# A streaming encoder's opening norm: the row scale moved from a ScalarE copy into the matmul that transposes the rows

## What is computed

```python
def _rms_norm(x, g):
    xf = x.astype(jnp.float32)
    y = xf * lax.rsqrt(jnp.mean(xf * xf, axis=-1, keepdims=True) + EPS)
    return (y * g.astype(jnp.float32)).astype(x.dtype)

h = _rms_norm(x, g_pre_mix)
z = h @ w_in
```

## Time and profile before

| what | us |
|---|---|
| median of 3 runs | 2531.35 |
| lowest and highest of them | 2529.56, 2534.56 |
| profiled execution, its own time | 2537.56 |
| its span in the trace | 2535.8 |
| third part of block 0 starts (end of the opening) | 41.41 |

### The profile page before, as it was taken

One profiled execution on the slowest core, in us unless ns is written; L12 is line 12 of the kernel. 1 busy time (PEld: TensorE's weight loads), 2 busy tenths in 40 slices (PEclk: granted clock), 3 DMA queues, 4 the chain that ended last, 5 costly groups with the idle time before them and its releaser, 6 DMA issues.

```text
span 2535.8 us, 37474 instructions
## 1 busy us (share of the span) xinstructions
PE 2475.6 (98%) x14264; PEld 2354.4 (93%) x14264; DVE 1158.1 (46%) x2297; ACT 674.4 (27%) x1365; POOL 490.3 (19%) x729
## 2 busy tenths in 40 slices
PE   7999999999999999999999999999999999999998
PEld 6999999999989999999999999988899898898996
DVE  4052425233366556557656435555343343343335
ACT  5122222323222222222222322323022131131221
POOL 1021201121165445446436000001000000000000
PEclk9999999999999999999999999999999999999999
DMA  4252625353423313322422634322011021110114
GB/s 160 90 183 73 222 78 180 119 172 122 138 76 132 126 58 123 128 85 95 136 96 97 219 124 133 100 91 83 25 59 42 25 66 33 33 58 25 49 41 157
DMA packets 219182, 256.88 MB, mean 101 GB/s; under 512 B 8256, under 2 KB 186816, under 8 KB 218944
## 3 DMA queue, kind: packets, MB, share of 16 engines
q1 hardware_dynamic: 219072, 255.37, 30.6%
HBM read 175.12 MB, written 80.22 MB: 101 GB/s over the span
## 4 chain that ended last, share of the span: by engine, by line
PE 70%; issue 12%; DVE 12%; DMA 2%; POOL 2%; ACT 1%; SPq 1%; DVEq 0%; POOLq 0%; ACTq 0%
PE bank L596 9%; PE bank L598 9%; PE bank L597 9%; PE bank L826 5%; PE bank L828 5%; PE bank L827 5%; PE bank L896 5%; PE bank L897 5%; PE bank L895 5%; PE bank L747 3%; DVE QE L1377 2%; DVE PP L1380 2%; PE bank L854 1%; PE bank L855 1%; PE bank L856 1%
## 5 line engine op out<-in xcount | busy, mean ns | idle before, releaser
L596 PE MATMUL bank<-XH,WHI 128*128 128x384 f32 x2304 | 791.6, 344 | 9.9 <-DVE XL L1242 4.3
L598 PE MATMUL bank<-XH,WLO 128*128 128x384 f32 x2304 | 774.2, 336 | 0.0
L597 PE MATMUL bank<-XL,WHI 128*128 128x384 f32 x2304 | 774.1, 336 | 0.0
L596 PEld LDWEIGHTS bank<-XH,WHI 128*128 128x128 f32 x2304 | 436.6, 190 | 16.0 <-ACT XH L911 6.2
L597 PEld LDWEIGHTS bank<-XL,WHI 128*128 128x128 f32 x2304 | 436.3, 189 | 0.9
L598 PEld LDWEIGHTS bank<-XH,WLO 128*128 128x128 f32 x2304 | 435.4, 189 | 0.0
L911 ACT ACTIVATE ZST<-bank 128x384 f32<-128x384 f32 x240 | 117.9, 492 | 566.3 <-PE bank L598 564.5
L826 PE MATMUL bank<-XH,WHI 128*128 128x384 f32 x768 | 257.7, 335 | 3.6 <-ACT XH L911 3.6
L828 PE MATMUL bank<-XH,WLO 128*128 128x384 f32 x768 | 257.2, 335 | 0.0
L827 PE MATMUL bank<-XL,WHI 128*128 128x384 f32 x768 | 257.2, 335 | 0.0
L1212 DVE TENSOR_TENSOR WLO<-WRAW,WHI 128x1024 fp32r<-128x1024 f32 x128 | 157.5, 1231 | 210.3 <-ACT WHI L911 205.0
(11 more groups left out here) (173 smaller groups left out, 3230.2 us busy)
## 6 DMA issues: line engine op xcount, KB each, us to landing
scratch_z<-ZST SPq DMA_DIRECT2D x80, 576.0 KB, 2.8
WRAW<-in_w_in SPq DMA_DIRECT2D x80, 512.0 KB, 3.9
HZ<-scratch_z SPq DMA_DIRECT2D x32, 576.0 KB, 5.2
WRAW<-in_w_up SPq DMA_DIRECT2D x32, 512.0 KB, 4.1
WRAW<-in_w_down SPq DMA_DIRECT2D x32, 512.0 KB, 3.3
MG<-scratch_z SPq DMA_DIRECT2D x16, 576.0 KB, 5.7
ZQ<-scratch_z SPq DMA_DIRECT2D x4, 1152.0 KB, 6.6
ZK<-scratch_z SPq DMA_DIRECT2D x4, 1152.0 KB, 8.6
```

What stands on the lines that cost most here:

```text
L596: pe.matmul(psum[c][:, 0:CH], WHI[p][:, k, :], XH[:, k, s], start=(k == 0), stop=False)
L597: pe.matmul(psum[c][:, 0:CH], WHI[p][:, k, :], XL[:, k, s], start=False, stop=False)
L598: last = pe.matmul(psum[c][:, 0:CH], WLO[p][:, k, :], XH[:, k, s], start=False, stop=(k == KT - 1))
```

## The change

For the opening norm the scaled copy of the rows (HR, 128 x 1024, ACT) is gone. In its place DVE multiplies the identity by the tile's reciprocal roots, one per partition, which gives a diagonal matrix (DGR, 128 x 128), and PE multiplies the unscaled rows by it: rows as the stationary operand, the diagonal as the moving one, an ordinary fp32 matmul with start and stop where `transpose` stood. Eight matmuls per tile, as before eight transposes. The DVE instruction stands first in its iteration, ahead of the next mean square, and takes over the two waits that the copy on ACT had (for rsc, and for the transposes of tile tt-2). The second norm passes no diagonal and keeps its transposes.

```diff
--- before.py
+++ after.py
@@ -103,7 +103,7 @@
 
         p0 = ExitStack()
         XR = [sb(f"XR{i}", [P, D], F32, p0) for i in range(NT)]
-        HR = [sb(f"HR{i}", [P, D], F32, p0) for i in range(2)]
+        DGR = [sb(f"DGR{i}", [P, P], F32, p0) for i in range(2)]
         TM = [sb(f"TM{i}", [P, 4, P], F32, p0) for i in range(2)]
         SQJ = sb("SQJ", [P, D], F32, p0)
         p0.close()
@@ -572,7 +572,7 @@
 
         @block.tensor
         def _(pe):
-            def norm_transpose(tt, src):
+            def norm_transpose(tt, src, diag=None):
 
                 b = 3 + 2 * (tt % 2)
                 pe.wait_ge(n_hr, tt + 1)
@@ -581,7 +581,11 @@
                         pe.wait_ge(n_tm, 2 * (tt - 2) + g + 1)
                     for i in range(4):
                         k = 4 * g + i
-                        last = pe.transpose(psum[b + g][:, i * P:(i + 1) * P], src[:, k * P:(k + 1) * P], ident[:, :])
+                        out, rows = psum[b + g][:, i * P:(i + 1) * P], src[:, k * P:(k + 1) * P]
+                        if diag is None:
+                            last = pe.transpose(out, rows, ident[:, :])
+                        else:
+                            last = pe.matmul(out, rows, diag[:, :], start=True, stop=True, skip_group_check=True)
                     last.then_inc(n_tp, 1)
 
             def gemm(n, m, p, c, first=False, w=None, part=range(KT)):
@@ -604,7 +608,7 @@
                 pe.sem_inc(s, 1)
             pe.wait_ge(c_in, 48)
             for tt in range(NT):
-                norm_transpose(tt, HR[tt % 2])
+                norm_transpose(tt, XR[tt], DGR[tt % 2])
                 if tt in (3, 6):
                     pe.wait_ge(n_xh, 2 * tt)
                     pe.wait_ge(n_xl, 2 * tt)
@@ -945,11 +949,6 @@
             for tt in range(NT + 1):
                 if tt < NT - 1:
                     first_sq(tt + 1)
-                if tt < NT:
-                    act.wait_ge(n_rs, tt + 1)
-                    if tt >= 2:
-                        act.wait_ge(n_tp, 2 * (tt - 2) + 2)
-                    act.activation(HR[tt % 2][:, :], XR[tt][:, :], ACT.Copy, scale=rsc[:, tt:tt + 1]).then_inc(n_hr, 1)
                 if tt == 2:
                     whi_block(0, 0, 0, free=False)
                 if tt == 5:
@@ -1249,6 +1248,11 @@
                               ALU.subtract).then_inc(lb_ch, 1)
             norm_ms(0)
             for tt in range(NT + 1):
+                if tt < NT:
+                    dve.wait_ge(n_rs, tt + 1)
+                    if tt >= 2:
+                        dve.wait_ge(n_tp, 2 * (tt - 2) + 2)
+                    dve.tensor_scalar(DGR[tt % 2][:, :], ident[:, :], rsc[:, tt:tt + 1], None, ALU.mult).then_inc(n_hr, 1)
                 if tt < NT - 1:
                     norm_ms(tt + 1)
                 if tt == 3:
```

## The result

The changed kernel takes 2551.54 us (median of 5 runs, 2546.87 to 2555.13), the kernel before 2534.56 us (median of 5, 2529.56 to 2538.85). The ratio is 1.0072, 95% interval 1.0053 to 1.0091: slower by some 17 us, where 2531.8 was forecast and 2535.2 was the upper end. (Of the 19.7 us between 2551.54 and the forecast, 3.2 are that these five runs of the kernel before have a higher median than the three on which the forecast was built, 2534.56 against 2531.35.) The profiled execution took 2551.54 us, its span is 2549.8, 14.0 more than before.

What follows compares the result with a forecast made beforehand. PE was taken to bound the kernel from the opening on. Start +0.65, middle squares -1.73 and tail +1.32 and +0.27 summed to +0.5, nothing later; added to the median 2531.35 this gave 2531.8 us, range 2527.8 to 2535.2.

Steps and rivals of the forecast that it cites:

- The steady tile gains nothing: Opening's steady tiles: without ACT's copy, a loop through ACT and DVE still takes 3.14 us per tile, against 3.13.
- (a) The diagonal: New DVE work per opening tile: about 0.2 us to the next start, fitting into 0.34 us of idle time.
- (b) The matmuls: New PE work per opening tile: 16 steps of 0.11 instead of eight, 1.76 us instead of 0.88.
- Step 1: Start of the opening, to the fourth square: PE starts earlier but takes 16 steps, 12.76 instead of 12.11, +0.65 us.
- Step 2: Opening, fourth to ninth square: five loops and two low parts take 17.98 us instead of 19.71, -1.73.
- Step 3: Opening's tail, where PE is the bound: 12 transposes grow by 0.11 each, +1.32, and tile 8's second half adds +0.27.
- B: Faster rival in the opening: clock up with the first matmuls and staying up; -2.8 us, 2528.5; chance 0.14.
- C: Faster rival on PE in the opening: each new matmul recorded as one step like a transpose; -2.8, 2528.5; chance 0.04.
- Rival A: Slower rival: clock stays at 1.2 GHz until the first half part; +2.2, 2533.6, or 2539.4 with low tail; chance 0.15.
- The kept loss of 1.6: Around block 0's third part: eleven matmuls at the low clock lose 1.6 us, expected to remain but possibly vanish.
- Step 4: After the opening: loads shift with it, the third block's low part has 8 us of cover and costs nothing.
- any difference that arises after 60 us: Listed sign that the forecast is wrong: a time difference arising later than 60 us into the kernel.

Runs made afterwards that it cites:

- p1: Changed kernel, shifted as in a112u, with the diagonal made by GpSimd instead of VectorE; 2533.64 us in one run.
- p2: As p1, with the mean square of tile tt+1 also put between the TM and XL halves of tile tt-1; 2538.71 us in one run.
- b144u: Kernel before with 144 more TensorE instructions ahead of the norm, 140 of them jumped over and never executed; 2550.61 us, ratio 1.0065.
- b24: Kernel before with 24 executed semaphore increments ahead of TensorE's first wait; 2533.04 us, ratio 0.9995.
- b60u: Kernel before with TensorE code shifted by 60 instructions, 56 of them never executed; 2550.18 us, ratio 1.0065.
- a112u: Changed kernel with TensorE code shifted by 112 more instructions, 108 never executed, 256 in all against the kernel before; 2534.48 us, ratio 0.9997.
- aunroll2: Changed kernel with both head loops, retention and HGRN2, written out on TensorE; 2533.25 us, ratio 0.9999.
- aunroll: Changed kernel with the loop over the four retention heads written out on TensorE; 2533.52 us, ratio 0.9996.
- a112: Changed kernel with 112 executed semaphore increments ahead of TensorE's first wait, a shift of 256 in all; 2545.24 us, ratio 1.0041.
- b144: Kernel before with 144 executed semaphore increments ahead of TensorE's first wait; 2569.26 us, ratio 1.0134.

## Why the prediction was wrong

Point by point:

- **What bounds the kernel**: PE from the opening on. Right, and it is why a wait of PE's own issue shows in full.
- **The steady tile gains nothing**: right. 3.13 us before and after; p1 shows the loop without DVE's load, p2 that opening it shortens the tile.
- **(a) The diagonal**: taken as 0.2 us to the next start, measured 0.42 (duration 0.28 against an estimated 0.23). It still fitted, but only just: the 0.34 us of idle time is gone and nothing is left.
- **(b) The matmuls**: right in time. Two instructions each, 0.21 us a step while the clock was low and 0.11 after (ten in 13.80 to 15.08).
- **Step 1**: +0.65 forecast, +0.89 measured (13.00 against 12.11): PE started at 7.95 and not 7.85, and the second TM half at 11.73 and not 11.5. **Step 2**: -1.73 forecast, 13.00 to 30.90 is 17.90 against 19.71, -1.81. **Step 3**: +1.59 forecast; from the ninth square to the last part it is 11.21 us against 9.59, +1.62. The sum is +0.7 against +0.5, the last part at 42.11. The three steps are right as differences, but that the sum came out within 0.2 in this pair of profiles is in part luck. The starts of that part in other profiles of the same opening lie at 43.4 to 44.0 with the old norm (b144u, b24, b60u) and 43.6 to 44.2 with the new (a112u, aunroll2, aunroll), so a few tenths either way aren't to be had from one profile. Two of the rivals' sums are off by a tenth: with the second bank at 7.85 + 16 x 0.11 + 0.28 = 9.9, B's step 1 is -1.0, and C's -1.0 and -1.73 make -2.7.
- **The clock**: the new matmuls did raise it in the first tiles. Steps of 0.21 (six from 11.70 in 1.49 us, the last duration in it) turned to 0.11 before 13.8, where before it rose only in the first half part. Rival A didn't come in this profile. But the rule drawn from it, that transposes don't raise the clock, doesn't hold. With the old norm in b24 the tile behind the first 16 transposes (8.90 to 12.86) runs at 0.11 a step, where the kernel before took 1.97 us for it:

```profile
14.37 1.09 PE L585 MATMUL bank<-ident,HR 128*128 128x128 f32 x8 [1.51 <-ACT HR L958]
```

  The same is seen in b144u, and not in before and b60u. The clock was up there with nothing but transposes run. The rule of the Trainium skill that the prediction cites ("TensorE: Matmul & The Clock Gate", section "Part 4: PE-mode transpose": the transpose mode does not count as PE activity the way matmuls do) agrees with the kernel before and not with these two, and the measurement decides. In the four profiles of the new norm that start on time the clock was up by 13.8 as well; in three of them (a112u, aunroll, aunroll2) it then fell for a while in the first half part, which is most of why their third part starts later than 42.11.
- **The kept loss of 1.6**: it vanished in this profile, as the prediction allowed. The kernel after is 0.86 ahead behind it (ACT's first copy of a finished part, ZST, starts at 46.56 against 47.42), and loses 1.00 again at 159.85, in a wait for a low part (L1211). With the old norm b144u waits 0.76 at that place (162.40), with the new one a112u not at all, so this isn't the norm's doing.
- **Step 4 is the one that failed.** "After the opening. The loads that wait for it shift with it" took it that behind the opening everything is the same work at a shifted time. The prediction asked what the new matmuls cost in time, 16 steps for 8, and never where they stand: they are also 144 instructions ahead of a loop whose code was kept between its passes by a margin of 24 to 60. The sum has no term for that. The runs put +16 us in its place (b144u, b60u), and 0 for all the rest of the change (a112u).
- **The rivals**: none had this. All were about the opening, with a chance of 0.07 for slower. The page showed 74 instruction packets, and the stretch of 300 to 690 us with a single one, which was there to be asked. Its last sign of being wrong, "any difference that arises after 60 us", is the one that came.

What the runs leave open: how many blocks are kept, and by which rule one is given up. That it depends on a seventh fetch point inside the loop fits eight kernels (before, b24, a112, a112u without loss; after, b60u, b144, b144u with it), but the point itself is only known to lie between 2481 and 2517. One number bears on it: the kernel after fetches 27 packets more than a112u (102 against 75), nine in each of the three passes, and 9 x 256 = 2304 instructions.

The Trainium skill, "Runtime: NRT & Kernel Launch", section "Instruction fetch mechanics", says that instructions are fetched ahead in blocks of 256, that TensorE holds 2048, and that a taken branch to code outside the window waits for a fetch. The runs agree with the block (1.21 MB in 74 packets are 16.4 KB) and with the wait (3.0 to 3.7 us). The loop of 1701 is under 2048 and still lost its start at two of the five shifts tried (60 and 144; not at 0, 24 and 256); the nine blocks of a pass are more than the eight that 2048 make, which would explain it, but no run tries that number. The same section says that only two blocks are held. Here the measurement decides against it: in three heads of the kernel before one packet was fetched, so that all of the loop was there.

## What to carry to other kernels

An edit on an engine that runs a loop has two prices, the time of its instructions and their place: an instruction added ahead of a loop shifts it against the blocks in which code is fetched, and a loop near the limit can then be fetched again in each pass (here at shifts of 60 and 144, not at 24 and 256). Look at the instruction packets in a stretch of the loop and for waits ended by "issue" at its start; if a change elsewhere in the program brings them, try it with unexecuted filler ahead of the loop, or with the loop written out, before judging the change. The second lesson is smaller: a busy engine freed of work gains nothing while a loop through two engines in fixed order has the same length.

## What the runs showed of the hardware that was not expected

- A jump back to code that is gone makes PE wait 3.0 to 3.7 us, and in the profile the granted clock is 0.50 behind such a wait (276 to 280 us in the kernel after); together 4.3 to 6.1 us per pass. Fetches of the same code in straight order cost nothing that can be measured (aunroll).
- The loss is all or nothing: 0 at a shift of 24, 16 us at 60 and at 144, 0 again at 256.
- A semaphore increment on PE takes its queue 0.153 us (23.25 against 18.36 us for PE's first matmul with 144 and 112 of them); 24 of them hide ahead of the first one, which starts at 8.90.
- Transposes alone can be followed by the full clock: 16 of them from 8.90 in b24, and the next eight take 1.09 us and not the 1.97 of the kernel before.
- A 128x128 scaling on DVE has a duration of 0.28 us, but the next instruction starts 0.42 after it.
